# Another starting place for the buffers of the rounded products in a two-block transformer kernel

## The reference

```
proj = rmsnorm(x) @ w_in                                   # first block
x = x + (sigmoid(ga) * (attn @ w_a) + sigmoid(gb) * (ssd @ w_s)) @ w_out
x = x + cross_attention(rmsnorm(x), rmsnorm(mem), ...)
x = x + square(relu(rmsnorm(x) @ w_up)) @ w_down
x = rmsnorm(x)
parts = rmsnorm(x) @ w_in_2                                # second block
x = x + (gate_a * (o_a @ w_proj_a) + gate_b * (o_b @ w_proj_b)) @ w_out
x = rmsnorm(x + hier_moe(rmsnorm(x)))
```

## The kernel before

| operand (stage) | before | after |
|---|---|---|
| weights pair, ring (all projections) | 128 | 128 |
| `xP1`, first projection of the first block | 320 | 128 |
| `hP1`, attention stage and state-space loop | 256 | 128 |
| own weights of the state-space loop, two of three parts | 256 | 128 |
| decay rows (`wP` stage at 301 us), moving | 192 | 128 |
| halves of the merge, `halfP`, `mergedP` | 256 | 128 |
| cross attention: `xP`, and the pairs after it | 448, 0, 256 | 128 |
| feed-forward: `hP`, `upT` | 256 | 128 |
| second block: `xP2`, `hP` | 256 | 128 |
| join: rows of `bP` / `aP` | 256 / 128 | 128 |
| join, `outP`: hi / lo | 128 / 256 | 128 |
| experts: weights and rows | 0 | 128 |

## Time and profile before

### The profile page before, as it was taken

How to read it: one execution, slowest core, us unless ns; L and a number is a source line. 1 busy time by engine, 2 the same in 40 slices (tenths; PEclk the granted TensorE clock), 3 DMA queues, 4 the chain that set the end, 5 groups by cost and what they waited for, 6 DMA issues and landing times.

```text
span 2430.9 us, 32383 instructions
## 1 busy us (share of the span) xinstructions
PE 2235.2 (92%) x11925; PEld 1869.3 (77%) x11925; DVE 1404.1 (58%) x2174; ACT 1081.8 (44%) x1863; POOL 345.0 (14%) x431
## 2 busy tenths in 40 slices
PE   6999989999997999889999999999989998969997
PEld 5888768888886787668888888987778886757774
DVE  4657435777776565553443435758646656456665
ACT  4445534666665423442322323654333344245553
POOL 1000001112111000000000000853334440012001
PEclk8999999999998999999999999999989999969999
DMA  5222422232221613223223143131010014259995
GB/s 193 86 76 32 96 90 65 59 90 61 74 60 56 234 44 104 76 97 104 87 88 103 35 157 104 36 109 66 27 44 1 1 39 170 109 203 395 415 414 196
DMA packets 169179, 273.23 MB, mean 112 GB/s; under 512 B 9865, under 2 KB 142297, under 8 KB 159193
## 3 DMA queue, kind: packets, MB, share of 16 engines
q1 hardware_dynamic: 164585, 255.22, 31.0%
q0 software_dynamic: 4464, 16.25, 1.8%
HBM read 240.00 MB, written 31.46 MB: 112 GB/s over the span
## 4 chain that ended last, share of the span: by engine, by line
PE 78%; DVE 8%; ACT 7%; DVEq 3%; issue 2%; DMA 1%; POOL 1%; POOLq 1%; ACTq 0%; SPq 0%
PE ps L178 19%; PE ps L179 18%; PE ps L180 18%; PE ps L3630 3%; ACT pair L364 1%; PE ps L3040 1%; DVE pair L370 1%; PE ps L3057 1%; PE ps L1119 1%; PE ps L1661 1%; PE ps L3594 1%; PE ps L1637 1%; PE ps L3008 1%; PE ps L2638 1%; PE ps L1097 1%
## 5 line engine op out<-in xcount | busy, mean ns | idle before, releaser
L180 PE MATMUL ps<-pair,pair 128*128 128x512 f32 (+1 forms) x2216 | 804.5, 363 | 0.0
L178 PE MATMUL ps<-pair,pair 128*128 128x512 f32 (+1 forms) x1960 | 731.7, 373 | 48.5 <-DVE pair L370 14.5
L179 PE MATMUL ps<-pair,pair 128*128 128x512 f32 (+1 forms) x1960 | 732.2, 374 | 0.0
L180 PEld LDWEIGHTS ps<-pair,pair 128*128 128x128 f32 x2216 | 422.4, 191 | 68.9
L178 PEld LDWEIGHTS ps<-pair,pair 128*128 128x128 f32 x1960 | 374.4, 191 | 113.7 <-issue 34.2
L179 PEld LDWEIGHTS ps<-pair,pair 128*128 128x128 f32 x1960 | 375.5, 192 | 68.1 <-issue 7.2
L370 DVE TENSOR_TENSOR pair<-ring,pair 128x2048 fp32r<-128x2048 f32 x95 | 219.0, 2305 | 139.0 <-ACT pair L364 138.8
L364 ACT ACTIVATE pair<-ring 128x2048 fp32r<-128x2048 f32 x102 | 194.6, 1908 | 202.5 <-PE ps L180 194.1
L880 DVE TENSOR_TENSOR arena<-ps,arena 128x512 f32<-128x512 f32 x56 | 38.7, 690 | 137.8 <-PE ps L180 137.8
L178 PE MATMUL ps<-part,pair 128*128 128x512 f32 x256 | 104.1, 407 | 11.8 <-DVE part L423 6.1
L1842 DVE SCALAR_TENSOR_TENSOR arena<-arena 128x512 f32<-128x512 f32 x128 | 97.8, 764 | 25.1 <-issue 12.1
(11 more groups left out here) (551 smaller groups left out, 3788.8 us busy)
## 6 DMA issues: line engine op xcount, KB each, us to landing
ring<-in_w_in SPq DMA_DIRECT2D x54, 1024.0 KB, 6.5
arena<-in_w_exp_down SPq DMA_DIRECT2D x23, 1024.0 KB, 10.9
ring<-in_w_up SPq DMA_DIRECT2D x16, 1024.0 KB, 5.4
ring<-in_w_down SPq DMA_DIRECT2D x16, 1024.0 KB, 5.1
ring<-in_w_exp_gate SPq DMA_DIRECT2D x16, 1024.0 KB, 8.9
ring<-in_w_exp_up SPq DMA_DIRECT2D x16, 1024.0 KB, 10.9
expert_results<-arena SPq DMA_DIRECT2D x22, 512.0 KB, 11.3
ring<-in_w_in SPq DMA_DIRECT2D x16, 512.0 KB, 6.0
```

The costliest lines, as they stand in the source:

```text
L178: nc.tensor.matmul(out, lhs[1], rhs[0], start=start, stop=False)
L179: nc.tensor.matmul(out, lhs[0], rhs[1], start=False, stop=False)
L180: return nc.tensor.matmul(out, lhs[0], rhs[0], start=False, stop=stop)
```

## The change

Seven places round up to 128 words (`P`, 512 bytes) where they rounded to 8 words (or assert the new multiple): `take_pair` and with it all pairs that it places, the start of the activations `xT` and `hT`, the decay rows, the halves of the merge and the join. The arena grows by 128 words to hold the gaps. The multiple is counted from the arena's start, so in the memory the buffers begin 128 bytes past a multiple of 512, all of them alike. The instructions, their order and their waits are the same on all five engines; only addresses differ.

```diff
--- before.py
+++ after.py
@@ -78,7 +78,7 @@
         self.ps = ctx.enter_context(nc.psum_tensor("ps", [P, 8, BANK], F32))
         self.ring = ctx.enter_context(nc.sbuf_tensor("ring", [P, 2, 4096], F32))
         self.ring_rounded = nc.alloc_sbuf_tensor_at("ring_rounded", [P, 2, 4096], F32R, offset=nc.sbuf_base - 4 * 8192)
-        self.arena_size = 44800
+        self.arena_size = 44928
         self.arena = ctx.enter_context(nc.sbuf_tensor("arena", [P, self.arena_size], F32))
         self.arena_at = nc.sbuf_base - 4 * self.arena_size
         self.top = 0
@@ -107,7 +107,7 @@
 
 
         size = 2 * chunks * n
-        self.top = -(-self.top // 8) * 8
+        self.top = -(-self.top // P) * P
         assert self.top + size <= self.arena_size, (self.top, size)
         t = self.nc.alloc_sbuf_tensor_at(f"pair_{self.pairs}", [P, 2, chunks, n], F32R,
                                          offset=self.arena_at + 4 * self.top)
@@ -127,7 +127,7 @@
         pair = Pair.__new__(Pair)
         parts = []
         for at in (hi_at, lo_at):
-            assert at % 8 == 0
+            assert at % P == 0
             parts.append(self.nc.alloc_sbuf_tensor_at(f"part_{self.pairs}", [P, chunks, n], F32R,
                                                       offset=self.arena_at + 4 * at)[:])
             self.pairs += 1
@@ -761,7 +761,7 @@
         two_gains = core.take(DC)
         one_and_gain = core.take(DC, 2)
         final_root = core.take(NT)
-        core.top = -(-core.top // 8) * 8
+        core.top = -(-core.top // P) * P
         x_at = core.top
         xT = core.take(DC, T)
         hT = core.take(DC, T)
@@ -2262,7 +2262,7 @@
             f_end = core.top
             hP = core.pair_at(x_at, DC, T)
             xP2 = core.pair_at(mark, DC, T)
-            assert mark + 2 * DC * T <= mark + NT * (QKV + AH * AD) and mark % 8 == 0
+            assert mark + 2 * DC * T <= mark + NT * (QKV + AH * AD) and mark % P == 0
             (s_par, s_a, s_g, s_sums, s_exp, conv_ready, feat_ready, s_turned, tok_ready, sq_ready,
              v_ready, root_ready, s_tap) = (
                 sem(f"delta_{n}") for n in ("parameters_landed", "a_log_exp",
```

## The result

| | median us | runs | ratio to before, 95% interval |
|---|---|---|---|
| before | 2429.83 | 5 | |
| after | 2415.49 | 5 (2415.12 to 2422.41) | 0.9943 [0.9918, 0.9967] |
| predicted | 2398 (2390 to 2414) | | |

What follows compares the result with a forecast made beforehand. TensorE's three matmul lines of `product`, 55% of the chain, were taken as the bound. Gains of 25.9 (512 columns) + 6.8 (256 columns) - 3.2 (waits) = 29.5 us took the median from 2428.04 to 2398 us, range 2390 to 2414.

Steps and rivals of the forecast that it cites:

- The class of products and the direction: Rounded products on TensorE: equal operand starts cut 512-column distances to 226.6 ns; 4848 of 5496 can gain.
- The modulus: Operand starts of TensorE's products count by their remainder modulo 512 bytes.
- Rival 3: Addresses modulo 512 have no part, or a true multiple of 512 counts, which the change misses: 2428 us; chance 0.05.
- rival 4: Equal starts make moving reads and weight loads collide; every product takes 240 ns, 37 us more, 2465 us; chance 0.03.
- The 256-column term: 2016 products of 256 columns drop to 113.3 ns: 10.1 us gain, 6.8 after the part hidden by GpSimd.
- the cover by GpSimd: Last features projection: TensorE's saving only lengthens its wait for GpSimd, from 3.81 to about 7 us; 3.3 us lost.
- The bounds: Distance of 256-column products after the change: at least 112 ns, at most 118.6, which is no gain.
- Rival 1: Only 512-column products gain; for 256 columns the weight load decides: 2405 us; chance 0.18.
- The 512-column term: 4848 products drop to 226.6 ns: 26.9 us gain, less 1.0 for half clock, 25.9 us.
- Cuts for waits: Stages where TensorE waits for other work: 2.2 us off for attention and scores, 1.0 for the state-space loop.
- Rival 2: Other engines take the gain back at hand-overs, above all in loop and attention; half remains, 2413 us; chance 0.07.

Runs made afterwards that it cites:

- e3: The kernel after, with the feed-forward's two activation pairs begun 128 bytes later, as in the kernel before: 2429.09 us, 0.9984 of before.
- e6: The kernel after, with the weights pair alone moved 64 bytes further: 2435.96 us, 1.0026 of before.
- e7: The kernel after with 256-byte multiples, and xP1 (hP1, second block's hP) and the memory's pair begun 64 bytes further: 2412.24 us, 0.993 of before.
- e4: The kernel after, unchanged, measured once more: 2416.86 us, 0.9951 of before.
- e2: The kernel before, with the weights pair alone moved from 128 to 256 bytes past a multiple of 512: 2422.11 us, 0.997 of before.
- e5: The kernel after, with multiples of 64 words (256 bytes) in place of 128: 2418.87 us, 0.9953 of before.
- e8: A bench without the model, TensorE alone: products with alternating starts, one odd start in three, plain float32 and bfloat16; alternating stationary starts take 233.3 ns.
- e1: A bench without the model, TensorE alone: rounded products, 48 for each pair of starts; equal starts take 226.6 to 227.2 ns at 512 columns.

## Why the prediction missed

By its own steps, against the profiled spans (forecast -29.5 us, found -17.2):

- **The class of products and the direction: right for 512 columns.** Equal starts give 226.6 ns; undoing it in e3 brings 232.5 back and e6 makes it worse. The modulus, 512 in the prediction, is 256, which changes nothing here. Rival 3 (addresses have no part) and rival 4 (equal starts are the costly ones) are out for 512 columns.
- **The 256-column term: this is the step that failed.** It stood at 10.1 us of gain, 6.8 after the cover by GpSimd, and measured +3.0 us of loss, summed over the stretches in which these products stand close together. That is 9.8 of the 12.3 us by which the forecast missed. I had written that no stretch had equal starts with 256 columns, and then took half of the 512-column distance, because the loop's mean fitted one product at 113.3 and two at 120.2. Any number pairs with some other to a given mean; 113.3 was in that fit because I had put it there. (Why the loop had 117.9 before, with two equal starts of three, no bench reproduces: 256 columns with one odd start were not run.) The bounds were wrong as well: "above, 118.6, no gain" left out a loss, though equal starts were as unseen there as any other.
- **Rival 1** (only 512 columns gain; 2405) was right that 256 columns do not gain, with a reason that e7 refutes: the weight load does not hold these products at 118, since e7 has long stretches of them at 113.3 ns with the same loads at another start.
- **The 512-column term, 25.9 us: 21.3 measured** in close stretches. The long one gave what it should, 3168 x (232.4 - 226.7) = 18.1 of 18.4. Missing are 0.8 us in the loop, where products of 512 and 256 columns alternate with others (2.7 instead of 3.6, by its mean of 227.9), and 0.5 us in the expert stage: its pairs went from 0 to 128 and its 552 products from 228.2 to 229.1 ns on the mean, for a reason that no run shows. Most of the rest of the 4.6 us is attention and scores, for which the forecast had its cuts: there the mean went from 231.97 to 230.95 ns and from 232.2 to 229.2.
- **Cuts for waits, 3.2 us: one pair of profiles can't judge them.** On its face 17.2 of the 18.3 us that the products gained (21.3 - 3.0) arrive in the span, so the cuts look 2 us too high. But the profiled execution before spent 195.7 us at half clock and the one after 186.3, and 9.4 us less of that is worth about 4 us (worked out below). Without this luck some 13 us arrive, in line with the medians, and the cuts were rather too small. Rival 2, half taken back at hand-overs, gave nearly the right time, 2413, for a wrong reason: TensorE's idle time grew by 2.1 us (195.7 to 197.8, the span without its busy time), not by half of 29.5.
- **GpSimd's cover:** the mechanism was right, as e7 shows, but with a loss in place of the gain there was nothing to cover; the wait went from 3.81 to 3.55 us.

**What moved besides.** The same work falls at other moments under the granted clock. Windows of the kernel before and then of the kernel after over the same four stretches (us, busy PE, PEld, DVE, ACT, POOL with counts, granted clock, DMA share, GB/s):

```profile
1507.00:1525.40 18.40, 15.91 (x132) 15.73 (x133) 10.40 (x30) 10.27 (x20) 0.00 (x0) 1.00 0.19 59
1525.40:1638.00 112.60, 107.20 (x831) 103.15 (x831) 68.91 (x82) 64.89 (x121) 85.52 (x107) 0.98 0.25 78
1638.00:1790.00 152.00, 142.06 (x720) 111.39 (x720) 102.05 (x213) 61.82 (x132) 44.20 (x55) 0.99 0.14 48
1900.00:1950.40 50.40, 46.59 (x376) 44.59 (x374) 30.89 (x39) 16.72 (x30) 20.75 (x16) 0.93 0.00 1
```

```profile
1487.80:1507.70 19.90, 17.55 (x132) 17.38 (x133) 10.43 (x30) 10.20 (x20) 0.00 (x0) 0.91 0.18 54
1507.70:1622.00 114.30, 109.15 (x831) 104.92 (x831) 68.46 (x82) 64.94 (x121) 86.05 (x107) 0.97 0.24 77
1622.00:1776.20 154.20, 144.26 (x719) 114.19 (x718) 101.66 (x213) 61.87 (x132) 44.35 (x55) 0.97 0.15 52
1885.70:1933.00 47.30, 43.47 (x377) 41.68 (x375) 30.94 (x40) 16.72 (x30) 20.82 (x16) 1.00 0.01 1
```

The first three cost 1.5, 1.7 and 2.2 us more after the change, with lower clocks beside them, and the last gives 3.1 back, at 1.00 instead of 0.93. A part of the first two is the dearer 256 columns (768 products by 1.3 ns, 1.0 us); beside the rest stand the lower clocks. The time at half clock, twice the missing share of the mean clock times the span, is 195.7 us before, 186.3 after and 193.2 in the same kernel again (e4). So it wanders by some 7 us between two executions of one program, and a single pair of profiles can't place a few us.

**What stays open.** Law sum and median agree in direction everywhere but for e3, whose median can't be told from before, but not in size when the kernel before is the base:

| | law sum minus before | median minus before |
|---|---|---|
| after, e4 | -21.4 | -14.3, -12.5 |
| e2 | -17.7 | -7.3 |
| e3 | -12.6 | -0.3 |
| e5 | -21.4 | -10.5 |
| e6 | +3.4 | +6.6 |
| e7 | -28.6 | -17.1 |

Between the variants the law fits better (e6 minus e4 19.1 for 24.8, e7 minus e4 -4.6 for -7.2, e2 minus after, not measured side by side, 6.6 for 3.7). Against the kernel before all of them are some 3 to 12 us dearer than the law says. The runs show two parts of this. First, the close stretches of the two traces give 18.3 us where the law sum has 21.4; attention and scores alone, where the products stand among others, gained 1.6 us where it has 4.4. (For e7 the law has 113.8 ns for 1824 products that took 115.6, 3 us.) Second, every run lists its mean granted clock. By it the kernel before spent 188 and 184 us at half clock on the mean of its runs beside e2 and e4, and the changed versions 189 to 197. Within each kernel the runs with more of it are the longer ones, by 0.42 us for each us, over 101 runs. So the 5 to 13 us more are worth an estimated 2 to 5 us, against every version alike. Together the two bring the kernel after to about 15 us of gain, where 12 to 14 were measured. Why the changed versions spend more time at half clock no run shows, and no run holds it fixed, so this part is a correlation.

## What to carry to other kernels

Where products in the rounded float32 follow each other without a gap, give moving and stationary operand the same start modulo 256 bytes for 512 columns, and let the moving one start 192 bytes past the stationary for 256 columns (115.6 ns on the mean in e7, for 119.9 with equal starts); one buffer on the wrong start is enough to lose it all. Never halve a price to get that of a half-sized operation: the part that does not scale may be the very one that the change acts on. And where the trace has no row for the state that a change creates, the range has to include a loss there.

## What the runs showed of the hardware

- The distance of rounded float32 products depends on the difference of the operands' starts modulo 256 bytes: 226.7 to 233.3 ns with 512 columns, 113.3 to 120.0 with 256, 173.3 to 176.7 with 384, 200.0 to 204.1 with 448 (e8; there equal starts, 202.8, are not the cheapest), nothing with 320 (146.7, e8) and 128 (111.7, e1). This holds where all products of a stretch have the same difference; mixed starts give other means (e8).
- The order of the starts reverses between 512 and 256 columns. At a difference of 192 and 256 columns there are two values, 113.3 and 117.8 ns, and the starts do not choose between them: the same pairs of starts took the one in e1 and the other in e8, and within one stage of e7 the stream changes from one to the other and back. What sets it is open.
- Plain float32 (429.2 ns a pass of 512 columns) and bfloat16 (215.8 for 512, 109.2 for 256) do not depend on the moving operand's start (e8). The Trainium skill ("TensorE: Matmul & The Clock Gate", Back-to-back issue gap) gives N/2.4 + 2.5 ns, 215.8 for 512 columns and 109.2 for 256, for what it calls the isolated gap of one matmul: e8 agrees to the digit for a dense stream in bfloat16, and e1 contradicts it for the rounded float32, by 11 to 18 ns at 512 columns.
- The clock was at its lower level, 1.2 GHz, for 185.5 (e7) to 198.6 us (e2) of the profiled spans, whatever the starts, and stretches of it fell in other stages after the change than before.
